# Three places for rounded weights, an earlier round in each recurrence pair, and a prologue by token tiles

## What is computed

```python
xn = rms_norm(x, norm_w)
z  = einsum('btd,de->bte', xn, w_in)
zs_mix = zs + mu_shift * (zs_prev - zs)                 # token shift
w_raw = w0 + tanh(wd) @ w_up;  a = sigmoid(a0 + ad @ a_up)
S_t = S_{t-1} diag(w_t) + S_{t-1} (-kk_t)(kk_t a_t)^T + v_t k_t^T;  y_t = S_t r_t
y_r = (groupnorm(y) + (r.k.r_k) v) * silu(g_r)
o_att = merged attention over windows (128,1), (512,4), (2048,16), * silu(g_a)
y = x + concat(y_r, o_att) @ w_out
```

## Time and profile before

| | us |
|---|---|
| median of 3 runs | 1502.58 (1502.21 to 1502.62) |
| profiled execution | 1509.95 |
| its span, first to last instruction | 1508.2 |
| PE busy | 1449.4 (96%) |
| POOL busy | 568.1 (38%) |
| DVE busy | 687.6 (46%) |
| ACT busy | 518.5 (34%) |
| mean granted clock of PE, share of full | 0.989 |

### The profile page before, as it was taken

How to read it: one execution, slowest core, us unless ns; L and a number is a source line. 1 busy time by engine, 2 the same in 40 slices (tenths; PEclk the granted TensorE clock), 3 DMA queues, 4 the chain that set the end, 5 groups by cost and what they waited for, 6 DMA issues and landing times.

```text
span 1508.2 us, 34221 instructions
## 1 busy us (share of the span) xinstructions
PE 1449.4 (96%) x14669; PEld 1355.2 (90%) x14669; DVE 687.6 (46%) x1437; ACT 518.5 (34%) x856; POOL 568.1 (38%) x731
## 2 busy tenths in 40 slices
PE   4999999999999999999999999999999998899998
PEld 4998999999899898989999999989999887689998
DVE  3217475664747557474753435344263353400000
ACT  5234242422414233242412444444444354212221
POOL 1344141422424133241512434444334334944443
PEclk9999999999999999999998999999999999899999
DMA  6232040312204032130311853645636447244451
GB/s 205 58 93 66 13 123 12 95 50 72 73 9 117 22 84 61 37 102 15 100 50 37 199 133 85 163 101 131 143 93 158 109 110 204 83 122 135 119 155 57
DMA packets 251924, 143.08 MB, mean 95 GB/s; under 512 B 12077, under 2 KB 244846, under 8 KB 251246
## 3 DMA queue, kind: packets, MB, share of 16 engines
q1 hardware_dynamic: 228156, 125.90, 32.0%
q10 hardware_dynamic: 23618, 15.00, 3.4%
HBM read 125.36 MB, written 15.45 MB: 93 GB/s over the span
## 4 chain that ended last, share of the span: by engine, by line
PE 84%; DVE 6%; POOL 4%; ACT 2%; DMA 2%; issue 1%; SPq 0%; ACTq 0%; DVEq 0%; POOLq 0%
PE acc L462 58%; PE head_banks L878 3%; POOL WL L445 3%; PE head_banks L883 2%; PE head_banks L868 2%; PE head_banks L820 2%; DVE AREN L1516 2%; PE head_banks L1042 1%; PE head_banks L1022 1%; PE head_banks L1035 1%; PE head_banks L991 1%; PE head_banks L920 1%; PE head_banks L929 1%; ACT WH L436 1%; PE head_banks L946 1%
## 5 line engine op out<-in xcount | busy, mean ns | idle before, releaser
L445 POOL TENSOR_TENSOR WL<-WR,WH 128x256 fp32r<-128x256 f32 (+1 forms) x656 | 510.2, 808 | 881.9 <-ACT WH L436 877.8
L462 PE MATMUL acc<-XH,WH 128*128 128x260 f32 (+1 forms) x2624 | 579.4, 302 | 17.7 <-POOL WL L445 15.8
L462 PE MATMUL acc<-XH,WL 128*128 128x260 f32 (+1 forms) x2624 | 530.6, 284 | 0.0
L462 PE MATMUL acc<-XL,WH 128*128 128x260 f32 (+1 forms) x2624 | 530.2, 284 | 0.0
L462 PEld LDWEIGHTS acc<-XH,WH 128*128 128x128 f32 (+1 forms) x2624 | 406.2, 190 | 57.2 <-issue 26.8
L462 PEld LDWEIGHTS acc<-XL,WH 128*128 128x128 f32 (+1 forms) x2624 | 406.8, 189 | 0.0
L462 PEld LDWEIGHTS acc<-XH,WL 128*128 128x128 f32 (+1 forms) x2624 | 406.1, 189 | 0.0
L436 ACT ACTIVATE WH<-WR 128x1024 fp32r<-128x1024 f32 (+1 forms) x164 | 171.8, 1048 | 183.1 <-PE acc L462 175.1
L470 ACT ACTIVATE AREN<-acc 128x520 f32<-128x520 f32 (+1 forms) x82 | 49.2, 600 | 331.4 <-PE acc L462 328.7
L1817 DVE TENSOR_TENSOR AREN<-head_banks,AREN 128x512 f32<-128x512 f32 x16 | 11.1, 692 | 172.9 <-PE head_banks L1093 172.9
L1620 DVE TENSOR_TENSOR AREN<-AREN,head_banks 128x128 f32<-128x128 f32 x160 | 46.3, 289 | 33.3 <-PE head_banks L878 19.1
(11 more groups left out here) (229 smaller groups left out, 1608.1 us busy)
## 6 DMA issues: line engine op xcount, KB each, us to landing
WR<-in_w_in SPq DMA_DIRECT2D x128, 512.0 KB, 3.9
WR<-in_w_out SPq DMA_DIRECT2D x32, 512.0 KB, 6.0
out<-AREN ACTq DMA_DIRECT2D x32, 256.0 KB, 3.9
AREN<-in_cache_k_win SPq DMA_DIRECT2D x16, 384.0 KB, 8.3
AREN<-in_cache_v_win SPq DMA_DIRECT2D x16, 384.0 KB, 8.9
mix_scratch<-AREN ACTq DMA_DIRECT2D x16, 260.0 KB, 4.2
AREN<-in_x_prompt SPq DMA_DIRECT2D x4, 1024.0 KB, 7.8
AREN<-in_cache_k_win SPq DMA_DIRECT2D x8, 512.0 KB, 7.1
```

The lines of the kernel that those rows point to most:

```text
L445: rest = pool.tensor_tensor(WL[:, k % 2, j:j + 2, 0:M], WR[:, k % 4, j:j + 2, 0:M], WH[:, k % 2, j:j + 2, 0:M].bitcast(F32), ALU.subtract)
L462: mm = pe.matmul(acc[0:M, hf, 0:HT], w[:, k % 2, j, 0:M], x[:, kt, hf * HT:(hf + 1) * HT], start=(kt == 0 and n == 0), stop=(kt == KT - 1 ...
```

## The change

WH and WL get a third place; the half with running number n uses place n % 3, and the waits on s_half are one half looser. Every feed rounds one half further ahead, at unit u half u//8+2 instead of u//8+1, and the prologue and group 1 round up to half 9 (ACT after the group's loop, POOL in its first list). In `pair_a` feed("lora") stands ahead of the sigmoids on ACT and ahead of the gate on POOL, and the Sigmoid table is loaded at the end of the pair before (in pair 0 as before). The prologue takes x by token tiles: the identity and the norm weights are loaded first, the LORA weights ahead of the parameter rows; a tile is normalised, transposed in four groups of four blocks, weighted by DVE (`f`), rounded by ACT (`hi`); POOL takes the rests of tiles 0 and 1 and of the samples, DVE those of tiles 2 and 3; the transposes of parameter and shift rows go between the two LORA tiles. In `pair_b` DVE waits for the new key row ahead of the second product instead of the first. In the output projection the rounds of halves 1 and 4 move ahead, and the last cache loads are split among the loads of its weights. ARENA is smaller, and two buffers share a place with others. SP's loop over the recurrence pairs, and the tables BEHIND_A and BEHIND_B, stay as they are.

```diff
-        WH = sb("WH", [128, 2, 8, 128], F32R)
-        WL = sb("WL", [128, 2, 8, 128], F32R)
+        WH = sb("WH", [128, 3, 8, 128], F32R)
+        WL = sb("WL", [128, 3, 8, 128], F32R)
...
         def round_half(act, g, k, M=128):
             act.wait_ge(s_w[k % 4], (g + (k // 4 + 1)) * 16)
-            if not (isinstance(g, int) and 4 * g + k < 2):
-                act.wait_ge(s_half, g * 4 + (k - 1))
+            place = (4 * g + k) % 3
+            if 4 * g + k >= 3:
+                act.wait_ge(s_half, g * 4 + (k - 2))
...
             for u in span[name]:
-                if u % 8 == 1 and (ahead or u // 8 < 7):
-                    round_half(act, g, u // 8 + 1)
+                if u % 8 == 1:
+                    round_half(act, g, u // 8 + 2)
...
-                if u % 8 == 1 and (ahead or u // 8 < 7):
-                    rest_half(pool, g, u // 8 + 1)
+                if u % 8 == 1:
+                    rest_half(pool, g, u // 8 + 2)
...
+            lora_half = lambda k: w_view[:, 8 * (k % 2):8 * (k % 2) + 8,
+                                         3 * DR + LORA * (k // 2):3 * DR + LORA * (k // 2 + 1)]
+            for k in range(4):
+                load_half(sp, 0, k, lora_half(k))
             sp.wait_ge(p_dve, DVE_P.at(0, "zrow"))
...
-            for k in range(3):
-                load_half(sp, GROUP_C, k, wo_half(0, (0, 2, 1, 3)[k]))
-            caches(PAIRS - 1)
-            load_half(sp, GROUP_C, 3, wo_half(0, 3))
+            caches(PAIRS - 1, (0,))
+            for k in range(2):
+                load_half(sp, GROUP_C, k, wo_half(0, (0, 2)[k]))
+            caches(PAIRS - 1, (1,))
+            for k in range(2, 4):
+                load_half(sp, GROUP_C, k, wo_half(0, (1, 3)[k - 2]))
...
+            def rest_x(name, full, low, high):
+                pool.wait_ge(p_act, ACT_P.at(0, f"hi{name}"))
+                pool.tensor_tensor(low, full, high.bitcast(F32), ALU.subtract)\
+                    .then_inc(p_pool, POOL_P.one(f"lo{name}"))
+            rest_x("4", turned_s, XL[:, :, T:TT], XH[:, :, T:TT])
+            for t in range(2):
+                for q in range(4):
+                    rest_x(f"{t}{q}", turned(t, q), x_group(XL, t, q), x_group(XH, t, q))
             for k in range(4):
                 rest_half(pool, 0, k, LORA)
-            for k in range(9):
+            for k in range(10):
                 rest_half(pool, group_a(0), k)
...
+                feed("lora")
                 pool.wait_ge(a_act, ACT_A.at(i, "sgg"))
                 pool.tensor_tensor(GG, GG, Z[:, 3, 1:TT + 1], ALU.mult).then_inc(a_pool, POOL_A.one("gate"))
-                for name in ("lora", "kk", "tail", "bonus", "vec", *GRAMS):
+                for name in ("kk", "tail", "bonus", "vec", *GRAMS):
...
+            for n, (t, q) in enumerate(groups, 1):
+                pe.wait_ge(p_dve, DVE_P.at(0, f"xn{t}"))
+                if n >= 4:
+                    pe.wait_ge(p_dve, DVE_P.at(0, done_with[n - 4]))
+                for k in range(4):
+                    tr = pe.transpose(HB[:, n % 4, 128 * k:128 * (k + 1)],
+                                      XTOK[:, t, 128 * (4 * q + k):128 * (4 * q + k + 1)], ident)
+                tr.then_inc(p_pe, PE_P.one(f"x{t}{q}"))
+            for k in range(KT):
+                if k % 4 == 0:
+                    pe.wait_ge(p_pool, POOL_P.at(0, "lo13"))
+                    pe.wait_ge(p_dve, DVE_P.at(0, f"lo3{k // 4}"))
+                multiply_unit(pe, 0, k, LORA)
...
+            square_sums(4)
+            square_sums(0)
+            square_sums(1)
+            act.wait_ge(p_dve, DVE_P.at(0, "f4"))
+            act.activation(XH[:, :, T:TT], turned_s, ACT.Copy).then_inc(p_act, ACT_P.one("hi4"))
+            square_sums(2)
+            round_x(0)
+            square_sums(3)
+            round_x(1)
+            round_x(2)
             round_half(act, 0, 0, LORA)
             round_half(act, 0, 1, LORA)
...
+            round_x(3)
             round_half(act, 0, 2, LORA)
             round_half(act, 0, 3, LORA)
...
+            round_half(act, group_a(0), 9)
...
-                act.preload_act_table(ACT.Sigmoid)
+                if i == 0:
+                    act.preload_act_table(ACT.Sigmoid)
                 act.wait_ge(a_mix, DVE_M.at(i, "mix"))
                 act.activation(KSQ, M3[:, 1], ACT.Square, scale=P_["k_k"]).then_inc(a_act, ACT_A.one("ksq"))
+                feed("lora")
                 act.wait_ge(a_pe, PE_A.at(i, "lora"))
...
-                feed("lora")
                 feed("kk")
...
+                if not then_b:
+                    act.preload_act_table(ACT.Sigmoid)
                 feed("var")
...
-                    round_half(act, GROUP_C, 1)
...
                     round_half(act, GROUP_C, 3)
+                    round_half(act, GROUP_C, 4)
...
+            for t in range(3):
+                normed(t + 1)
+                weighted(t)
+            weighted(3)
+            for q in range(4):
+                for t in (2, 3):
+                    dve.wait_ge(p_act, ACT_P.at(0, f"hi{t}{q}"))
+                    dve.tensor_tensor(x_group(XL, t, q), turned(t, q), x_group(XH, t, q).bitcast(F32),
+                                      ALU.subtract).then_inc(p_dve, DVE_P.one(f"lo{t}{q}"))
...
-                dve.wait_ge(s_krow, done(1, i, 16))
                 for t, n in enumerate(TS):
                     if t:
                         after(f"rd{t - 1}")
+                    if t == 1:
+                        dve.wait_ge(s_krow, done(1, i, 16))
```

More of the change, by code:

```diff
@@ L286, in build @@
         SQJ = pro.take(D)
+        ROWN, NWC = pro.take(128), pro.take(KT)
         aa = Arena(AREN, ARENA_N)
@@ L363, in build @@
         YO, YOS = cc.take(2, 4, 128), cc.take(2, 128)
[L366 to L370, removed]
+        groups = [(t, q) for t in range(4) for q in range(4)]
+        xg = lambda s, t: [f"{s}{t}{q}" for q in range(4)]
+        PE_P = Steps(["nrow", "x4", *[f"x{t}{q}" for t, q in groups], "rows", "shift", "ltail"], ahead=False)
+        square = lambda t: [f"{s}{t}" for s in ("sq", "ln", "rs")]
+        ACT_P = Steps([*square(4), *square(0), *square(1), "hi4", *square(2), *xg("hi", 0), *square(3), *xg("hi", 1),
+                       *xg("hi", 2), *xg("hi", 3), "tanh", "ltail"], ahead=False)
+        DVE_P = Steps(["zrow", "bias", "pn", "xn4", "xn0", "f4", "xn1", *xg("f", 0), "xn2", *xg("f", 1), "xn3", *xg("f", 2),
+                       *xg("f", 3), *[f"lo{t}{q}" for q in range(4) for t in (2, 3)], "rows", "shift",
                        "lz", "ldiff", "lds", "lmix"], ahead=False)
+        POOL_P = Steps(["lo4", *xg("lo", 0), *xg("lo", 1)], ahead=False)
         last = LEVELS - 1
@@ L441, in rest_half @@
             pool.wait_ge(s_hi, g * 4 + (k + 1))
-            if not (isinstance(g, int) and 4 * g + k < 2):
-                pool.wait_ge(s_half, g * 4 + (k - 1))
+            place = (4 * g + k) % 3
+            if 4 * g + k >= 3:
+                pool.wait_ge(s_half, g * 4 + (k - 2))
             for j in range(0, 8, 2):
-                rest = pool.tensor_tensor(WL[:, k % 2, j:j + 2, 0:M], WR[:, k % 4, j:j + 2, 0:M],
-                                          WH[:, k % 2, j:j + 2, 0:M].bitcast(F32), ALU.subtract)
+                rest = pool.tensor_tensor(WL[:, place, j:j + 2, 0:M], WR[:, k % 4, j:j + 2, 0:M],
+                                          WH[:, place, j:j + 2, 0:M].bitcast(F32), ALU.subtract)
             rest.then_inc(s_lo, 1)
@@ L597, in cache_room, with caches @@
                 sp.wait_ge(o_tail, done(0, PAIRS, 32))
-            def caches(i):
-                if not isinstance(i, int) or i > 0:
-                    sp.wait_ge(b_dve, DVE_B.at(i - 1, "pr2"))
-                for n, (dst, view, s) in enumerate(((KC, kc_view, s_kc), (VC, vc_view, s_vc))):
-                    if n == 1 and (not isinstance(i, int) or i > 0):
-                        sp.wait_ge(b_pe, PE_B.at(i - 1, "av"))
+            def caches(i, parts=(0, 1)):
+                for n in parts:
+                    dst, view, s = ((KC, kc_view, s_kc), (VC, vc_view, s_vc))[n]
+                    if i > 0:
+                        if n == 0:
+                            sp.wait_ge(b_dve, DVE_B.at(i - 1, "pr2"))
+                        else:
+                            sp.wait_ge(b_pe, PE_B.at(i - 1, "av"))
                     cols = view.rearrange("s b (i c) -> s b i c", i=PAIRS)
@@ L723, in _ @@
                     rest_half(pool, GROUP_C, 2 + (k == 13))
+                if k == 14:
+                    rest_half(pool, GROUP_C, 4)
             for m in range(1, D // 256):
-                for k in range(4):
+                for k in range(1 if m == 1 else 0, 4):
                     rest_half(pool, m + GROUP_C, k)
@@ L764, in _ @@
                     pe.wait_ge(s_evac, 2)
+                    pe.wait_ge(s_const, 16)
+                    pe.wait_ge(p_dve, DVE_P.at(0, "rows"))
                     for j in range(2):
@@ L1443, in out_pair @@
```

(5 more changed lines are left out.)

97 lines of the change are left out of this document (52 added, 45 removed).

## The result

The changed kernel takes 1539.9 us (median of four, 1537.04 to 1542.06) against 1502.6 for the kernel before: ratio 1.0223, 95% interval 1.0201 to 1.0246. That is 37.3 us slower; the prediction was 1542. The profiled execution of the changed kernel took 1539.49, with a span of 1537.7.

What follows compares the result with a forecast made beforehand. PE's own order of work was taken to bound the kernel (busy 87.95 of 89.80 us). Terms 56.7 - 7.35 + 0.7 - 5.7 + 3.4 - 0.6 - 7.4 = +39.7 gave 1542 by medians, range 1518 to 1560.

Steps and rivals of the forecast that it cites:

- The stall: Pairs 0 to 6, unit 49: ACT's round waits for next group's first load, idling PE 5.4 us a pair.
- The clock behind it: After each 5.4 us gap PE's granted clock falls to 0.50, losing 2.7 us a pair (0 to 3.4).
- The 1.21 waits: Projection matmuls' waits for POOL's rests of weights go; 1.05 us kept in each of pairs 1 to 7, -7.35.
- The prologue: Up to group 1's start: unit 0 at 30.3, group 1 at 58.0 instead of 63.72, -5.7 us (-10.4 to -2).
- the port rule: Skill's exclusive DVE/GpSimd port lock: two DVE rests cost 2 x 1.29, prologue -4.0, whole 1544; a tenth of forecast's chance.
- the 2.6 allowed for handovers: Prologue: 2.6 us for three engines handing over block by block, moving unit 0 from 27.7 to 30.3.
- The first attention pair: Round at unit 9 waits for its load, delaying the key row's copy (5.3 us to land): +3.4 (0 to 6).
- The output projection: Waits of 1.68 (1.65 of it) and 3.06 go, with 2.7 of low clock: -7.4 us (-3 to -10).
- The rival without the stall: Next group's first load has landed when ACT asks at unit 49, so no stall: 1485 us, chance 0.10.

Runs made afterwards that it cites:

- e1: Changed kernel with the first load of each next group issued ahead of the sample states' load and store in SP's list: 1488.0 us, ratio 0.9872.
- e2: Changed kernel with half 8 in the recurrence pairs rounded and its rest taken at unit 57, with half 9, instead of unit 49: 1511.2 us, ratio 1.0014.
- e3: Changed kernel with the first two loads of each next group in reverse order: 1556.0 us, ratio 1.0323.
- e4_filler_20: Changed kernel with 20 further matmuls on PE ahead of the wait for ACT's copy of U, pairs 0 to 6: 1533.3 us, ratio 1.0192.
- e6: Changed kernel with all feeds rounding one half ahead as before, everything else as changed: 1485.4 us, ratio 0.9866.
- e7: Kernel before with only the recurrence pairs' feed("lora") ahead of sigmoids and gate and the Sigmoid table loaded a pair earlier: 1499.3 us, ratio 0.9957.
- e5: e1 with half 3's load (second attention group) before the last states' store, and half 9's round before group 1's last evacuation: 1483.1 us, ratio 0.986.
- e8: Changed kernel rounding one half ahead in recurrence pairs, two in attention pairs, half 3's load (second attention group) before the last states' store: 1482.9 us, ratio 0.985.

## Why the prediction was right, point by point

**The stall.** 5.4 was forecast for each of seven pairs, 5.25 to 5.33 are there. All its links were in the trace of before: ry, the store, the load, its landing of 6.0 (6.1 after), the round, the copy of U. e1 removes it by SP's order, e2 by the round's place, e3 makes it longer by the landing: all three ends of the explanation are shown.

**The clock behind it.** The mechanism holds (e4_filler_20), the size was too large: 2.7 forecast, 1.7 to 2.2 found. The row taken, had 5.35 us at the low level behind one gap of 3.06. In the seven pairs the low stretch differs from pair to pair, 3.3 to 6.2 us behind gaps of the same length, and so do the periods, 95.61 to 97.37; pair 1 has the longest of both.

**The 1.21 waits.** The size was right (1.05 forecast; e1's periods are 1.12 shorter in the mean), the reason given is not what it takes. The prediction put it down to the third place, "because the half is rounded and its rest taken a half ahead". e6 and e7 show that the feed's place ahead of the sigmoids and the gate, with the table load out of the way, is enough, with two places as well as with three. Whether rounding further ahead would do it without moving the feed, no run shows. Rounding two halves ahead even costs a little in these pairs (88.57 in e1 and e5 against 88.34 in e6 and e8); in the attention pairs it gains 0.22 to 0.28 each and 0.8 in the short one.

**The prologue** came out at -6.3 for -5.7: unit 0 began at 31.0, forecast 30.3, and the rest went a little faster. What came last there were POOL's rests of weights, so the two DVE rests of x on which the port rule was weighed did not set the start:

```profile
31.01 0.72 PE L482 MATMUL acc<-XH,WH 128*96 128x260 f32 x2 [5.29 <-POOL WL L465]
```

But DVE and POOL did hold each other up. The prediction read its rows as "both are slowed and neither stops"; this prologue shows the two taking turns (DVE and POOL, two stretches):

```profile
15.35 1.99 DVE L1530 TENSOR_SCALAR AREN<-AREN 128x2048 f32<-128x2048 f32 x1
16.21 2.27 POOL L700 TENSOR_TENSOR XL<-AREN,XH 128x512 fp32r<-128x512 f32 x1
```

```profile
27.35 1.08 DVE L1556 TENSOR_TENSOR XL<-AREN,XH 128x512 fp32r<-128x512 f32 x1
27.84 1.04 POOL L465 TENSOR_TENSOR WL<-WR,WH 128x192 fp32r<-128x192 f32 x1
28.35 1.07 DVE L1556 TENSOR_TENSOR XL<-AREN,XH 128x512 fp32r<-128x512 f32 x1
28.84 1.03 POOL L465 TENSOR_TENSOR WL<-WR,WH 128x192 fp32r<-128x192 f32 x1
```

The normalising of a tile takes DVE 1.29 in the kernel before. Here it ends 1.08 after the POOL rest that was running when it began (14.97 to 16.26), and the next POOL rest, 1.29 otherwise, ends 1.14 after it. In the second stretch each operation ends 0.45 to 0.55 after the other engine's; a DVE rest takes 1.07 instead of the 0.69 of the first, which began before POOL's rests of weights. Two of POOL's eight rests of x were held up by 0.97 each, and its first four rests of weights took 1.04 each, where four of 128x256 with DVE nearly idle took 0.71 each (284.15). Together that is about 3.2 of the 30.87 at which POOL was done; without it POOL would have ended at about the 27.7 that was forecast for it. That the 2.6 allowed for handovers covered most of this is luck. The Trainium skill (SBUF — State Buffer, section "SBUF: two separate sides") has an exclusive lock under which the loser blocks for the whole instruction, and these rows agree with it: in each case the later operation ends behind the other by most of the time that it takes alone (1.08 and 1.14 of 1.29; about 0.54 of DVE's 0.69 and 0.45 of POOL's 0.71). The 2 x 1.29 that the prediction worked out by it did not come, since the two DVE rests met POOL's short rests of weights and not its rests of x; 0.39 is what a DVE rest lost there, near the 0.43 that was counted.

**The first attention pair** came out at +2.8 for +3.4, and the closeness is luck. The chain was right, but one link was mis-sized: DVE could use the copied key row 2.7 after the copy's issue (883.62 to 886.31), not 5.3; in e4_filler_20 it was 5.2, and why it varies is not shown. So PE's wait was only 1.69. What made up for it was a term that the sum had at nothing, the clock behind the wait:

```profile
890.10 0.49 PE L1066 MATMUL head_banks<-AREN 64*128 64x128 f32 x4 [1.69 <-DVE AREN L1819]
```

```profile
891.20:894.50 3.30, 3.30 (x18) 0.50 0.19 38
```

Half of the 3.30, about 1.6, is lost there; 1.69 and 1.6, less the 0.3 by which every attention pair is shorter, come near the 2.8. e5, which moves the load and loses the wait, confirms the cause.

**The output projection** brought 4.3 instead of 7.4. The wait of 3.06 and the low clock behind it went. The wait of 1.68 at ACT's round is gone too, and PE comes to its next wait for DVE (L1059, now L1103) 46.1 after the last pair's first transposes, where it came after 47.7 before. That is the 1.65 in size, though other waits on the way changed too. But where before that wait was 2.26 and left the clock at 1.00, it is now 2.94, and the clock falls behind it:

```profile
1346.14 0.50 PE L1103 MATMUL head_banks<-CA,AREN 16*128 16x16 f32 x3 [2.94 <-DVE AREN L1876]
```

```profile
1346.14:1351.99 5.85, 5.85 (x38) 0.50 0.00 0
```

The longer wait costs 0.7 and half of the 5.85 at the low clock 2.9, a term that the forecast did not have and nearly all that is missing from its 7.4. This is read from the two traces; no run took it apart.

**The sum.** 39.7 forecast, 37.3 measured by medians. The errors were small and of both signs: low clock -4, tail +3, attention pairs -2; that they partly cancel is luck. The rival without the stall gave 1485. e1, which takes the stall away, measures 0.9872 of the kernel before, 1483 at the 1502.6 from which the forecast was made.

## What to carry to other kernels

When work is moved ahead, follow its inputs back to the queue that brings them: the consumer moved by half a step, the load behind a store in SP's list did not, and an engine that runs in order made everything behind the round wait for it. Ask for every wait removed which part of a change removes it: here the feed's new place, with the table load out of its way, did what the third place for weights was meant to do, and rounding two halves ahead, for which the third place was made, brought the loss. And price an idle gap of PE by more than its length: here what followed ran at half the clock for 3 to 6 us.

## What the runs showed of the hardware that was not expected

PE's granted clock fell to 0.50 in three executions with no gap before it, each time behind the stretch of a recurrence pair in which PE runs chains of products of 64x64 with 32 and 64 columns: in the kernel before at 794 (shown above), in e6 in one pair (91.43 instead of 88.4) and in e7 in one (91.62). In the other pairs of the same traces, with the same work, it did not fall there. It cost 3 to 6 us. Nor does the length of a gap alone decide: behind the 2.26 at 1313.32 the clock stayed at 1.00 in the kernel before, while behind the 1.69 at 890.10 in the changed kernel it fell, and behind the 2.29 in e1, at the same instruction as the 2.26, it was low for part of the next 7 us (PE's timeline and windows of e1):

```profile
1297.08 0.34 PE L1107 MATMUL head_banks<-CA,AREN 16*128 16x16 f32 x3 [2.29 <-DVE AREN L1880]
```

```profile
1297.08:1300.00 2.92, 2.92 (x29) 0.73 0.02 6
1300.00:1304.00 4.00, 4.00 (x35) 0.77 0.00 0
```

What decides it, the runs don't show.
